# Attention by pairs of heads inside a two-block transformer kernel: scores from partition halves, values into column halves, tables of distances on GpSimd

## The reference, cut to what matters

```python
HEAD_DIM = 64; N_HEADS = 8; SEQ = 512
DILATED_BRANCHES = ((128, 1), (512, 4), (2048, 16))

s = jnp.einsum('bhrnqd,bhrnkd->bhrnqk', qb, kc) * (HEAD_DIM ** -0.5)
bias = -slopes[:, None, None] * jnp.asarray(delta * dil, dtype=jnp.float32)
s = s + bias[None, :, None, None]
s = jnp.where(valid[None, None, None], s, -jnp.inf)
m = jnp.max(s, axis=-1); p = jnp.exp(s - m[..., None]); l = jnp.sum(p, axis=-1)
o = jnp.einsum('bhrnqk,bhrnkd->bhrnqd', p, vc.astype(jnp.float32))
...
# over the three branches: out = sum_i e^{m_i} o_i / sum_i e^{m_i} l_i
u = h @ w_in[l]; q, k, v, ga, gb = jnp.split(u, [...], axis=-1)
attn = dilated_attention(split_heads(q), split_heads(k), split_heads(v), slopes)
conv = conformer_conv(ga, gb, conv_w[l], conv_b[l], conv_ln_g[l], conv_ln_b[l])   # width 31, depthwise
mix = jnp.concatenate([attn, conv], axis=-1) @ w_out[l]
```

## Time and profile before

| | us |
|---|---|
| median of 3 runs | 2130.91 (2130.61 to 2132.85) |
| profiled execution, its own time | 2125.87 |
| its span | 2124.3 |
| outside the span | 1.6 |
| attention and convolution, 32 units | 196.2 to 292.6 |
| from there to the next stage's first work | 292.6 to 307.9 |

### The profile page before, as it was taken

The page is one execution under the profiler, slowest core; times in us unless marked ns, Lnnn a source line. Parts: engine busy times, 40 slices in busy tenths (PEclk is TensorE's granted clock), DMA queues, the critical chain, the costliest instruction groups (busy, mean ns, idle before and its releaser), DMA issues. The chain is left out here.

```text
span 2124.3 us, 28074 instructions
## 1 busy us (share of the span) xinstructions
PE 1941.0 (91%) x10255; PEld 1552.9 (73%) x10255; DVE 1276.3 (60%) x1747; ACT 1030.0 (48%) x1551; POOL 182.6 (9%) x192
## 2 busy tenths in 40 slices
PE   5999889499999999996399989989999989999997
PEld 4444444378888888885387559988999878999886
DVE  4435974689999999995724545744224644544433
ACT  2104751278888888884445644344322333332222
POOL 2001630121111111110110000000000000000000
PEclk8999999599999999998599999999999989999999
DMA  9257700399999999994521001011222212233320
GB/s 358 80 198 274 280 14 30 128 381 393 390 390 382 392 388 384 384 384 148 193 71 37 24 21 60 21 60 60 89 91 98 81 50 80 81 98 100 100 99 40
DMA packets 112081, 368.21 MB, mean 173 GB/s; under 512 B 6989, under 2 KB 61523, under 8 KB 99699
## 3 DMA queue, kind: packets, MB, share of 16 engines
q1 hardware_dynamic: 105090, 344.76, 43.9%
q0 software_dynamic: 6560, 22.02, 3.0%
q10 hardware_dynamic: 338, 0.13, 0.0%
HBM read 333.08 MB, written 33.82 MB: 173 GB/s over the span
## 5 line engine op out<-in xcount | busy, mean ns | idle before, releaser
L1315 DVE TENSOR_TENSOR weight_parts<-fixed,weight_parts 128x1024 fp32r<-128x1024 f32 x384 | 442.8, 1221 | 48.7 <-ACT weight_parts L1268 46.6
L1268 ACT ACTIVATE weight_parts<-fixed 128x1024 fp32r<-128x1024 f32 x384 | 374.5, 1067 | 27.2 <-DMA fixed<-in_w_exp_gate_dram 18.8
L1427 DVE TENSOR_TENSOR weight_parts<-fixed,weight_parts 128x1024 fp32r<-128x1024 f32 x135 | 162.5, 1222 | 215.2 <-ACT weight_parts L1419 215.1
L1528 PE MATMUL psum<-token_parts,weight_parts 128*128 128x264 f32 x720 | 210.8, 293 | 6.3 <-PEq L1749 3.3
L1528 PE MATMUL psum<-mix_parts,weight_parts 128*128 128x512 f32 (+3 forms) x656 | 206.9, 315 | 9.9 <-DVE weight_parts L1427 6.2
L1530 PE MATMUL psum<-token_parts,weight_parts 128*128 128x264 f32 x720 | 208.1, 289 | 0.0
L1529 PE MATMUL psum<-token_parts,weight_parts 128*128 128x264 f32 x720 | 207.9, 289 | 0.0
L1199 PE MATMUL psum<-weight_parts,token_parts 128*128 128x512 f32 x512 | 205.9, 402 | 1.9 <-DVE weight_parts L1315 1.9
L1529 PE MATMUL psum<-mix_parts,weight_parts 128*128 128x512 f32 (+3 forms) x656 | 207.4, 316 | 0.0
L1530 PE MATMUL psum<-mix_parts,weight_parts 128*128 128x512 f32 (+3 forms) x656 | 206.5, 315 | 0.0
L1201 PE MATMUL psum<-weight_parts,token_parts 128*128 128x512 f32 x512 | 200.7, 392 | 0.0
(11 more groups left out here) (419 smaller groups left out, 3539.0 us busy)
## 6 DMA issues: line engine op xcount, KB each, us to landing
fixed<-in_w_exp_gate_dram SPq DMA_DIRECT2D x32, 2048.0 KB, 10.5
fixed<-in_w_exp_up_dram SPq DMA_DIRECT2D x32, 2048.0 KB, 10.1
fixed<-in_w_exp_down_dram SPq DMA_DIRECT2D x32, 2048.0 KB, 9.3
fixed<-in_w_in_dram SPq DMA_DIRECT2D x26, 1024.0 KB, 5.2
fixed<-in_w_mod_dram SPq DMA_DIRECT2D x12, 2048.0 KB, 12.6
expert_rows<-fixed SPq DMA_DIRECT2D x8, 2560.0 KB, 25.5
fixed<-in_w_ffn_up_dram SPq DMA_DIRECT2D x11, 1024.0 KB, 5.3
fixed<-in_w_ffn_gate_dram SPq DMA_DIRECT2D x11, 1024.0 KB, 5.2
```

What stands on the lines that cost most here:

```text
L1268: act.activation(weights[:, 0, piece, :], ring[:, s, q * PIECE:(q + 1) * PIECE], ACT.Copy).then_inc(high_ok, 1)
L1315: dve.tensor_tensor(out, src, high_part.bitcast(F32), ALU.subtract).then_inc(done, 1)
L1427: dve.tensor_tensor(out, raw, high.bitcast(F32), ALU.subtract).then_inc(self.low_ok, 1)
L1528: pe.matmul(out, x(0), w(0), start=start, stop=False)
```

## The change

Three things change together.

1. The zero halves go. Keys are stored like the queries, two heads to a block (`kT`, 4 full copies, no memsets). The two heads of a pair are multiplied one right behind the other, one from partitions 0 to 63 and one from 64 to 127, into two banks. Units are renumbered: 8 units make a pair, and they alternate between its heads, with key widths 128, 128, 256, 256, 384, 384, 512, 512.
2. The values of a pair are one group of 8 matmuls that alternate between output partitions 0 to 63 and 64 to 127 of one bank. There are 4 such groups, in place of 8 groups of 4, in the third unit of the next pair, and 4 copies of 128 partitions in place of 8 of 64. `PT` is two buffers of a pair each, and the second one is slot 3 of the weight ring, which is free in this stage.
3. The head's table is made on GpSimd, in two instructions (distance times slope, plus count) in place of one on DVE. Four tables are made at the stage's start, ahead of GpSimd's first add, and two more at the start of the second and of the third tile.

```diff
-    g["kz"] = kz = arena[:, b:b + 4096].rearrange("p (h n) -> p h n", h=HEADS)
+    g["kT"] = kT = arena[:, b:b + 2048].rearrange("p (m n) -> p m n", m=4)
...
-            for h in range(HEADS):
-                lo = 64 * (1 - h % 2)
-                step(pool.memset(kz[lo:lo + 64, h, :], 0.0))
...
-                        act.activation(kz[0:64, 2 * m, :], src[0:64, :], ACT.Copy)
-                        act.activation(kz[64:128, 2 * m + 1, :], src[64:128, :], ACT.Copy).then_inc(taken, 1)
+                        act.activation(kT[:, m, :], src, ACT.Copy).then_inc(taken, 1)
...
-    PT = spare[:, 0:4096].rearrange("p (i j n) -> p i j n", i=2, j=4)
+    PT = [x.rearrange("p (i j n) -> p i j n", i=2, j=4) for x in (spare[:, 0:4096], g["ring"][:, 3, :])]
...
+    PAIR = 2 * TT
+
+    bias = g["ring"][:, 0, 0:4 * SEQ].rearrange("p (i n) -> p i n", i=4)
+    S_BANKS, O_BANK = ((0, 1), (5, 6)), 4
...
+    def unit(u):
+
+        pair, rest = divmod(u, PAIR)
+        i, r = divmod(rest, 2)
+        return pair, i, r, 2 * pair + r
+
+    s_bank = lambda u: S_BANKS[(u // 2) % 2][u % 2]
...
+            def table(h):
+                if h >= 4:
+                    pool.wait_ge(s_sb, PAIR * (h // 2 - 1))
+                pool.tensor_scalar(bias[:, h % 4, :], dist, -SLOPES[h], None, ALU.mult).then_inc(scaled, 1)
+                pool.wait_ge(scaled, h + 1)
+                pool.tensor_tensor(bias[:, h % 4, :], bias[:, h % 4, :], count, ALU.add).then_inc(table_ok, 1)
+
+            for h in range(4):
+                table(h)
             for m in range(CM):
+                if m in (1, 2):
+                    table(2 * m + 2)
+                    table(2 * m + 3)
...
             def scores(u):
-                h, i = divmod(u, TT)
+                pair, i, r, h = unit(u)
                 n = (i + 1) * P
                 off = SEQ - n
                 if i == 0:
-                    step(dve.scalar_tensor_tensor(out=bias[:, h % 2, :], in0=dist, scalar=-SLOPES[h], in1=count,
-                                                  op0=ALU.mult, op1=ALU.add))
+                    dve.wait_ge(table_ok, h + 1)
                 dve.wait_ge(s_ps, u + 1)
                 if u >= 2:
                     dve.wait_ge(e_ok, u - 1)
-                dve.tensor_tensor(sc[:, u % 2, 0:n], bias[:, h % 2, off:], psum[:, u % 2, 0:n], ALU.add).then_inc(s_sb, 1)
+                dve.tensor_tensor(sc[:, u % 2, 0:n], bias[:, h % 4, off:], psum[:, s_bank(u), 0:n], ALU.add).then_inc(s_sb, 1)
...
-            def take_out(h):
-                act.wait_ge(o_ps, h + 1)
-                lo = 64 * (h % 2)
-                act.activation(mixT[lo:lo + 64, h // 2, :], psum[0:64, 4 + h % 2, :], ACT.Copy).then_inc(o_sb, 1)
+                act.activation(PT[pair % 2][:, r, 0:i + 1, i * P:(i + 1) * P], src, ACT.Copy).then_inc(pt_sb, 1)
+
+            def take_out(pair):
+                act.wait_ge(o_ps, pair + 1)
+                act.activation(mixT[:, pair, :], psum[:, O_BANK, :], ACT.Copy).then_inc(o_sb, 1)
...
-            def scores(u):
-                h, i = divmod(u, TT)
-                if u >= 2:
-                    pe.wait_ge(s_sb, u - 1)
-                pe.matmul(psum[:, u % 2, 0:(i + 1) * P], qT[:, h // 2, i * P:(i + 1) * P], kz[:, h, 0:(i + 1) * P],
-                          start=True, stop=True).then_inc(s_ps, 1)
+            def scores(step):
+
+                if step >= 2:
+                    pe.wait_ge(s_sb, 2 * step - 2)
+                for u in (2 * step, 2 * step + 1):
+                    pair, i, r, h = unit(u)
+                    row = slice(HD * r, HD * r + HD)
+                    pe.matmul(psum[:, s_bank(u), 0:(i + 1) * P], qT[row, pair, i * P:(i + 1) * P], kT[row, pair, 0:(i + 1) * P],
+                              start=True, stop=True).then_inc(s_ps, 1)
...
-            def values(h):
-                pe.wait_ge(pt_sb, TT * (h + 1))
-                if h >= 2:
-                    pe.wait_ge(o_sb, h - 1)
+            def values(pair):
+                pe.wait_ge(pt_sb, PAIR * (pair + 1))
+                if pair:
+                    pe.wait_ge(o_sb, pair)
                 for j in range(TT):
-                    last = pe.matmul(psum[0:64, 4 + h % 2, j * P:], v[:, j, h * HD:(h + 1) * HD],
-                                     PT[:, h % 2, j, j * P:], start=(j == 0), stop=(j == TT - 1))
+                    for r in range(2):
+                        h = 2 * pair + r
+                        last = pe.matmul(psum[HD * r:HD * r + HD, O_BANK, j * P:], v[:, j, h * HD:(h + 1) * HD],
+                                         PT[pair % 2][:, r, j, j * P:], start=(j == 0), stop=(j == TT - 1))
                 last.then_inc(o_ps, 1)
...
-                if u + 1 < UNITS:
-                    scores(u + 1)
+                if u % 2 == 0 and u + 2 < UNITS:
+                    scores(u // 2 + 1)
                 if u < UNITS:
                     conv_taps(u)
                 if u >= 2:
                     turn(u - 2)
-                    if (u - 2) % TT == 0 and u - 2 > 0:
-                        values((u - 2) // TT - 1)
-            values(HEADS - 1)
+                    if (u - 2) % PAIR == 0 and u - 2 > 0:
+                        values((u - 2) // PAIR - 1)
+            values(HEADS // 2 - 1)
```

More of the change, by code:

```diff
@@ L564, in weigh @@
             def weigh(u):
-                h, i = divmod(u, TT)
-                n = (i + 1) * P
+                n = (unit(u)[1] + 1) * P
                 dve.wait_ge(e_ok, u + 1)
@@ L587, in exps @@
             def exps(u):
-                n = (u % TT + 1) * P
+                n = (unit(u)[1] + 1) * P
                 act.wait_ge(mx, u + 1)
@@ L640, in _ @@
                     take_probs(u - 2)
[L641 to L643 removed]
+                    if (u - 2) % PAIR == 1 and u - 2 > PAIR:
+                        take_out((u - 2) // PAIR - 1)
+            take_out(HEADS // 2 - 1)
             for m in range(CM):
                 act.wait_ge(cent, m + 1)
[L646 removed]
+                act.activation(PT[0][:, 0, m, :], mixT[:, 4 + m, :], ACT.Square).then_inc(sq, 1)
         @block.tensor
         def _(pe):
[L650 to L655 removed]
+            def scores(step):
+                if step >= 2:
+                    pe.wait_ge(s_sb, 2 * step - 2)
+                for u in (2 * step, 2 * step + 1):
+                    pair, i, r, h = unit(u)
+                    row = slice(HD * r, HD * r + HD)
+                    pe.matmul(psum[:, s_bank(u), 0:(i + 1) * P], qT[row, pair, i * P:(i + 1) * P], kT[row, pair, 0:(i + 1) * P],
+                              start=True, stop=True).then_inc(s_ps, 1)
             def turn(u):
[L658 removed]
+                _, i, _, _ = unit(u)
                 pe.wait_ge(pw, u + 1)
@@ L705, in _ @@
                 pe.wait_ge(sq, m + 1)
-                last = pe.matmul(psum[:, 7, :], ones, PT[:, 0, m, :], start=(m == 0), stop=(m == CM - 1))
+                last = pe.matmul(psum[:, 7, :], ones, PT[0][:, 0, m, :], start=(m == 0), stop=(m == CM - 1))
             last.then_inc(var_ps, 1)
```

16 lines of the change are left out of this document (4 added, 12 removed).

## The result

The changed kernel takes 2145.07 us (median of 4 runs, 2143.01 to 2146.64); before, 2130.76 in the same session. The ratio is 1.0077, 95% interval 1.0064 to 1.009: slower by 14 to 19 us. The forecast was 2127.0, and its range ended at 2139.

A forecast was written before the change was run, and what follows sets the result against it. DVE was taken as the bound, PE close behind. First tile -0.1, second and third -1.2 each, fourth -1.9, end +0.5 sum to -3.9 us: 2130.9 to 2127.0, range 2121 to 2139.

The forecast's parts named there:

- The chain from `c_sum`: PE's work in a tile after L541 ends: 14.8 us with halves side by side, 17.5 one after another.
- two taps and four transposes, twice: First part of PE's chain in a tile, put at 4.3 us.
- The prediction named the clock: A clock falling in the tiles, where it was 1.00, was listed among what would make the prediction wrong.
- I take side by side: Array halves overlap on PE: a pair's values 2.6 us, two scores 1.0 and 1.3, tile 22.9.
- Rival 1's main form: Halves run one after another, pair's values 4.6 us, deciding from 3.4: +8.1 us, 2139.0; chance 0.26.
- The small version of rival 1: Switching between whole and half arrays costs PE about 0.15 us, 0.45 a tile: 2128.5 in place of 2127.0.
- I take 0.7: GpSimd's multiplication for a head table takes 0.7 us, between 0.55 and 1.52; a table 2.1.
- rival 2: GpSimd takes back DVE's relief: 3.1 us tables, first tile 3.8 us late, total -0.5, 2130.4; chance 0.18.
- The first tile, -0.1: GpSimd's four tables delay its adds, yet the first tile ends where it did: -0.1 us.
- The reading of DVE: Removing two L555 a tile takes 2.45 us off DVE's work in each tile.
- DVE comes first, PE close behind it: In each tile DVE is busy longest, 22.5 to 23.2 us, then PE, 20.4 to 22.0.
- The end, +0.5: After the last tile, two heads' values side by side take 4.5 us in place of one's 3.99.

The follow-up runs named there:

- e_order_only: Kernel before with only the unit order changed to pairs of heads, both heads' values in one block; 2146.18 us, ratio 1.0085.
- e_turn: Order by pairs alone in the kernel before, plus a unit's transposes ahead of the next taps on PE; 2140.87 us, ratio 1.0064.
- e_warm: Order by pairs alone in the kernel before, plus three unread matmuls in each of a pair's two widest units; 2141.39 us, ratio 1.0055.
- e_split: Order by pairs alone in the kernel before, with the second head's values moved to the next pair's seventh unit; 2139.81 us, ratio 1.0048.
- n_early: Kernel before with unpadded keys, scores over 64 rows, and six head tables made by DVE in the input projection; 2135.47 us, ratio 1.0043.
- b_tables_pool: Kernel before with only the head tables moved to GpSimd, on the changed kernel's schedule; 2132.70 us, ratio 1.0026.
- a_tables_dve: Changed kernel with the head tables back on DVE; 2136.64 us, ratio 1.0044 to the kernel before.
- w_warm: Changed kernel with three unread matmuls added in each of a pair's two widest units; 2136.51 us, ratio 1.0042 to the kernel before.
- y_early8: Kernel before with all eight head tables made by DVE in the input projection, transposed probabilities in the free weight-ring slot; 2124.47 us, ratio 0.9981.
- f_rows: Kernel before with unpadded keys and scores over 64 rows, one unit at a time; 2135.33 us, ratio 1.0031.

## Why the prediction was wrong

**The chain from `c_sum`, 14.8 us a tile: this step failed.** It gave "two taps and four transposes, twice (4.3 us)". In the fourth tile they take 6.97 us (279.93 to 286.90): +1.84 for the first taps and +0.42 for the first transposes at the lower clock, +0.3 and +0.1 for the second ones. Behind that lies a tacit step: I added PE's and DVE's work as if one followed the other with nothing waiting, and never asked where PE is idle. In the pairs' order the narrow units stand together where PE has its taps, and the wide ones where it has none. So each engine waits in turn for the other, and PE's idle time brings the clock down. The prediction named the clock as what would make it wrong, but gave that no chance and no price. That the order costs as much as the whole loss, e_order_only shows (+18 us), and e_turn, e_warm and e_split each take back a part of it. (The +0.1 of the second transposes isn't the clock's, which was back at 1.00 from 285.0 us on.)

**"I take side by side": right.** The values of both heads start within 0.01 us of each other (235.74 and 235.75 in the second tile), and a pair's take 2.30 us (290.17 to 292.47), where I gave 2.6 and one after another would be 4.6. Both heads' scores of 384 columns take 0.85 us (286.90 to 287.75), where I gave 1.0: the two run fully beside each other, not in 9 of 16 or 3 of 4 steps. Rival 1's main form, from its point of 3.4 us on, didn't happen; its side, slower, came by another way.

**The small version of rival 1 (0.15 us for a change of height) was mis-sized.** It is 0.4 us a group of scores, by n_early against the earlier trace rows. The Trainium skill, TensorEngine Tiling (Array Packing), section Key Properties, says that a change of tiling mode drains the engine; the trace agrees, with about 0.1 us more at each edge of the group. Another 0.1 us stands between its two passes, where the mode doesn't change. In pairs two scores of 512 columns with these gaps are 1.06 + 0.2 us, before 1.72: half of the 0.86 that the overlap saves is gone.

**"I take 0.7" for GpSimd's multiplication: wrong, beyond my upper bound of 1.52 too.** It has a mean of 1.65 us, a table takes 3.0, not 2.1, and the first add began at 208.34, not 204.7. The Trainium skill (GPSIMD Engine Reference, section 4.1 Engine selection) has two-input operations about twice as slow there as on VectorE and one-input ones roughly at line rate; the trace agrees on the first, 1.38 us for the add after DVE's 0.68 for one of this size (L547), but here the one-input multiplication is the slower one of the two, 1.65 us, and the measurement decides. That is the table of rival 2 (3.1 us), whose balance, -0.5 us, counted on DVE's relief in the later tiles: b_tables_pool measures +5.5 us, and none of its later tiles is shorter.

**The first tile, -0.1: it was +5.4.** This is a second step that failed, and it is the tables': with them back on DVE the tile is 24.6 us (a_tables_dve), with them on GpSimd in the old order 3.7 us longer (b_tables_pool), and the order of the pairs alone costs nothing there (24.6 in e_order_only). DVE's two waits for tables, 2.9 and 2.2 us, come to 5.1; the sum had the first as 2.1 and set it against the L555 that went. The fallen clock (0.84) isn't the cause: w_warm has 0.94 and the same 30.4 us.

**The reading of DVE, 2.45 us a tile for L555: half right.** With the tables out of the stage altogether the second and third tile of y_early8 are still 24.1 us. "DVE comes first, PE close behind it" took DVE for a bound that gives way by what is taken off it. Only with the transposes ahead of the taps do the tiles come to 22.5; the prediction's sum for DVE alone gives 21.7 without GpSimd's tables.

**The end, +0.5: it was +1.8.** A pair's values take 4.47 us there, where I had worked out 4.5, but that is luck: the factor of 9/8 didn't hold (the passes ran fully beside each other), and the clock stood at its lower level for all of them, while before it had fallen to that level only from 295.0 us on, for 3.4 us. They also start later behind the last unit (2.8 us, after 2.1), and the first part of the mean behind them is at the lower clock as well:

```profile
310.26 4.53 PE L692 MATMUL psum<-fixed,first_block_memory 128*64 128x512 f32 x16 [0.69 <-ACT fixed L618]
314.73 4.15 PE L723 MATMUL psum<-first_block_memory,fixed 128*128 128x512 f32 x8
```

**Input projection, 0: right** (PE 88.00 of 88.00 us busy, as before, and the next stage begins at 196.11 us, after 196.20).

Still open: how the order's 18 us divide exactly, since the three edits overlap; why the clock fell in f_rows, where PE had been idle for only 1.15 us, when it stayed at 1.00 behind 1.25 us in the kernel before (219.71); and what the halves are worth in an order that suits both engines.

## What to carry to other kernels

When a change reorders work over two engines, lay both engines' loads unit by unit side by side, before and after: equal sums say nothing if the heavy units of the one meet the light ones of the other. An idle stretch on PE can be paid twice, by the wait and by the granted clock behind it. Where engines wait for each other in a loop, time taken off the busiest one comes through only as far as the others' order lets it: here the tables made in a stage where DVE had time gave 0.19%, and two tiles shrank only when PE's order changed as well. When a change brings a new order with it, its order alone is the first experiment to run.

## What the runs showed of the hardware

- Matmuls of two column halves, and of two row halves, with fp32 operands run beside each other: starts 0.01 us apart, two heads' values in 2.30 us, the time of one.
- Going between scores over 64 rows and matmuls over 128 costs PE about 0.1 us at each edge, and as much between a half-height matmul's two passes: 0.4 us a group of scores (n_early, 222.73 to 226.13 us).
- GpSimd's TENSOR_SCALAR of 128x512 fp32 takes 1.49 to 1.81 us (mean 1.65 in the changed kernel), its two-operand add for the tables 1.26 to 1.69, a memset of 64x512 0.69.
- In the changed kernel the granted clock fell to the 1.2 GHz level at each border of tiles (into the fourth tile 0.9 us behind an idle stretch of 3.47 us on PE, for 6.8 us, 278.1 to 284.9); in the first tile it fell once more, at 213.3, behind 2.51 us of idle time. Matmuls that nothing reads, put into the gap, kept it at 1.00 in the tiles 2 to 4 and took 7.5 us off the whole.
